# Attention: one plain 32-bit product for the second half of the probabilities in two of nine steps

## The chip, the core and the metric

The kernel runs on one core of a Trainium2 chip. The metric is the device time of one execution in microseconds. The engines are named as the profile names them: PE (matmuls, PEld its weight loads), DVE (VectorE), ACT (ScalarE), POOL (GpSimd) and SP (SyncE, which here only issues DMAs).

## What is computed

One layer of a hybrid network over 2048 latent and 256 context tokens: a projection, a gated linear attention (GLA) and a softmax attention side by side, an output projection, and a feed-forward block. The change is in the softmax attention, which the reference computes like this, with 8 query heads, 2 key/value heads (so 4 query heads share one) and a head size of 64:

```python
def blocked_attention(q, k, v):
    ...
    def one_block(qi):
        s = jnp.einsum('bqhgd,bkhd->bhgqk', qi.astype(F32), k.astype(F32))
        p = jax.nn.softmax(s, axis=-1)
        return jnp.einsum('bhgqk,bkhd->bqhgd', p, v.astype(F32))
```

Latent queries read 2048 latent and 256 cached keys; context queries read the 256 context keys. Everything is in 32-bit floats.

## The kernel before

The stages run one after the other; attention takes the stretch from about 280 to 1095 us. Its work is cut into units: one tile of 128 query tokens and one key/value head, so that 4 heads x 128 tokens = 512 columns (`ROW`) go through at once. There are 32 latent units and 4 context units. A latent unit has nine steps (`NS`), numbered j = 0 to 8 in the code and first to ninth here; a step takes two key tiles of 128 keys, its two halves, i = 0 and 1. Line numbers in this section are those of the kernel before.

Precision is kept by splitting. A number is rounded to a shorter format (fp32r) and the rest is kept as a second number. Keys and queries are split that way, and `vals` holds in its 128 columns the rounded values (64) and their rests (64). The probabilities are split while the kernel runs. For each step:

- PE makes the scores of each half in two products (L840, L841) into one of three banks `p_s`.
- ACT takes the exponential of each half into `prob` (L945, 128 x 512), then rounds both halves in one instruction into `thi` (L950, 128 x 1024).
- POOL subtracts: `tlo` = `prob` - `thi` (L781, 128 x 1024). In the third and the seventh step (`FOLDED`) it first adds the two halves of `prob` into `fold` (L779).
- DVE adds the probabilities up in `p_sum` (L1017, L1020), one step behind the scores: two adds in most steps, one (of `fold`) in the folded ones.
- PE multiplies the values with `thi` and with `tlo` (L854, L855) into `p_o`, for each half, three steps behind the scores: the products of the third step are issued in the sixth, those of the seventh in the first step of the next unit.

`prob`, `thi` and `tlo` have six slots (`SLOTS_P`), so a slot comes round after six steps. Beside this PE computes for the next unit the maxima over the keys in 18 "pieces" (L805, and L811 for the 256 cached keys), which DVE reduces (L993, L996) from two banks `p_r` used in turn; the plan of how many pieces go with which step is a list of numbers (`PLAN`). The same two banks serve the transposes of the maxima (L820), the row sums (L875, of which DVE takes the reciprocal, L1043) and their spread over the columns (L868). When a unit's products are done, in the third step after it (the fourth of the next unit), ACT copies half of `p_o` to `osb` (L930), and DVE adds the halves (L1039). In the sixth step of some units (`CHUNK_STEP`) PE also computes a piece of the modulation (L898).

Each engine works through its instructions in the order of the code and waits on semaphores. On PE a step is: scores of half 0, transposes and sums if due, values of half 0, a piece, scores of half 1, a piece, values of half 1, what pieces are left, the chunk.

Of the kernel before, what the change touches and what calls it, by code (L numbers as in the profile page):

```python
# [7 lines left out]
F32 = mybir.dt.float32  # L8
F32R = mybir.dt.float32r
U32 = mybir.dt.uint32  # L10
ALU = mybir.AluOpType
ACT = mybir.ActivationFunctionType
# [544 lines left out]
def attention(nc, g):  # L557
# [11 lines left out]
    ROW = 4 * P  # L569
# [6 lines left out]
    PLAN_FIRST = [3, 2, 1, 2, 2, 3, 3, 2, 0]  # L576
    AHEAD = 2
    FOLDED = (2, 6)
    BANKS = 3
    ADDS = 2 * NS - len(FOLDED)  # L580

# [8 lines left out]
    with ExitStack() as stack:  # L590
        ph = Phase(nc, stack, "att")
        s = ph.s
# [11 lines left out]
        prob = ph.sb("prob", [P, SLOTS_P, 2 * ROW])  # L604
        thi = ph.sb("thi", [P, SLOTS_P, 2 * ROW], F32R)
        tlo = ph.sb("tlo", [P, SLOTS_P, 2 * ROW], F32R)
# [16 lines left out]
        p_o = [ph.ps("p_o0"), ph.ps("p_o1")]  # L623
# [19 lines left out]
        def adds_before(b, j, i):  # L643

            folded = sum(1 for f in FOLDED if f < j) if b.nds > 1 else 0
            return b.a0 + (2 * j - folded + i)

        def bank_of(b, j, i):
            return p_s[(2 * b.step_no[j] + i) % BANKS]

# [77 lines left out]
        with nc.Block() as block:  # L728
# [40 lines left out]
            @block.gpsimd  # L769
            def _(pool):  # L770
                def step(S):
                    if S.now:
                        e, j = S.now
                        sl = e.step_no[j] % SLOTS_P
                        if e.nds > 1 and j in FOLDED:
                            f = FOLDED.index(j)
                            pool.wait_ge(s.ex, (e.g0 + (j + 1)) * 2)
                            wait(pool, s.sum, adds_before(e, j, 1) - ADDS)
                            pool.tensor_tensor(fold[:, f, :], prob[:, sl, 0:ROW], prob[:, sl, ROW:2 * ROW], ALU.add).then_inc(s.fold, 1)  # L779
                        pool.wait_ge(s.hi, e.g0 + (j + 1))  # L780
                        pool.tensor_tensor(tlo[:, sl, :], prob[:, sl, :], thi[:, sl, :].bitcast(F32), ALU.subtract).then_inc(s.lo, 1)  # L781

                schedule(step)

            @block.tensor
            def _(pe):
                pe.wait_ge(s.ckl, 1)
                for t in range(2):
                    for n in range(4):
                        last = pe.transpose(p_s[t][:, n * P:(n + 1) * P],  # L790
                                            ckp[:, t, n // 2, 2 * (n % 2):2 * (n % 2) + 2, :].rearrange("p a d -> p (a d)").bitcast(F32),
                                            g.ident[:, :])
# [30 lines left out]
                def step(S):  # L823
                    for v, i, item in S.early:
                        piece(v, i, item)
                    late = S.now and S.now[0].nds > 1
                    if S.turn and not late:
                        turn(*S.turn)
                    pieces = list(S.max)

                    def scores(i):
                        e, j = S.now
                        half = (e.g0 + j) * 2 + i
                        if j == 0 and i == 0:
                            pe.wait_ge(s.aux, e.n + 1)
                            pe.wait_ge(s.q[e.q], e.q_round * 32 + 32)
                        wait(pe, s.ex, half - (BANKS - 1))
                        bank = bank_of(e, j, i)
                        kt = slice((e.kt0 + 2 * j + i) * P, (e.kt0 + 2 * j + i + 1) * P)
                        pe.matmul(bank[:, :], g.keysT[:, e.kv, 0, kt], qa[:, e.q, :], start=True, stop=False)  # L840
                        pe.matmul(bank[:, :], g.keysT[:, e.kv, 1, kt], qb[:, e.q, :], start=False, stop=True).then_inc(s.st, 1)  # L841

                    def values(i):
                        b, j = S.val
                        if i == 0:
                            pe.wait_ge(s.lo, b.g0 + (j + 1))
                            if j == 0:
                                wait(pe, s.osum, b.n - 1)
                                if S.after is not None:
                                    pe.wait_ge(s.mod, S.after[0] * 2 + (S.after[1] + 1))  # L850
                        sl = b.step_no[j] % SLOTS_P
                        v = g.vals[:, (b.kt0 + 2 * j + i) * KVH + b.kv, :]
                        cols = slice(i * ROW, (i + 1) * ROW)
                        pe.matmul(p_o[b.kv][:, :], v, thi[:, sl, cols], start=j == 0 and i == 0, stop=False)  # L854
                        last = pe.matmul(p_o[b.kv][:, :], v, tlo[:, sl, cols], start=False, stop=j == b.nds - 1 and i == 1)  # L855
                        if i == 1:
                            last.then_inc(s.pv, 1)

                    if S.now:
                        scores(0)  # L860
                    if S.turn and late:
                        turn(*S.turn)
                    if S.turn_sums:
                        b, (bank, before) = S.turn_sums
                        pe.wait_ge(s.lb, b.n + 1)
                        pe.wait_ge(*before)
                        for n in range(2):
                            last = pe.transpose(bank[:, n * P:(n + 1) * P], lb[:, 2 * n:2 * n + 2, :].rearrange("p h d -> p (h d)"), g.ident[:, :])  # L868
                        last.then_inc(s.tsums, 1)
                    if S.fin:  # L870
                        b, (bank, before) = S.fin
                        pe.wait_ge(s.sums_out, b.n + 1)
                        pe.wait_ge(*before)
                        for h in range(G4):
                            last = pe.matmul(bank[:, h:h + 1], sums[:, b.kv, h * P:(h + 1) * P], ones[:, 0:1], start=True, stop=True)  # L875
                        last.then_inc(s.ls, 1)
                    if S.val:
                        values(0)
                    if pieces:
                        piece(*pieces.pop(0))  # L880
                    if S.now:
                        scores(1)
                    if len(pieces) > 1:
                        piece(*pieces.pop(0))
                    if S.val:
                        values(1)
                    for p in pieces:
                        piece(*p)
                    if S.chunk is not None and S.now[1] == CHUNK_STEP:

                        (e, j), (c, half) = S.now, S.chunk
                        wait(pe, s.osum, e.n)
                        pe.wait_ge(s.aw, c * 16 + 16)
                        pe.wait_ge(s.cpad, 1)
                        for k in range(KC):
                            for q in range(4):
                                col = half * HALF + q * QUART
                                last = pe.matmul(p_o[1 - e.kv][q * COLS:(q + 1) * COLS, 0:QUART], cpad[:, k, :], aw[:, k, col:col + QUART],  # L898
                                                 start=k == 0, stop=k == KC - 1)
                        last.then_inc(s.chunk, 1)  # L900
# [4 lines left out]
            def _(act):  # L905
# [11 lines left out]
                def step(S):  # L917
# [3 lines left out]
                    if S.summed:  # L921
                        b = S.summed
# [3 lines left out]
                    if S.fin:  # L926
                        b = S.fin[0]
# [3 lines left out]
                    if S.store:  # L931
                        b = S.store
                        act.wait_ge(s.oo, b.n + 1)
                        act.dma_start(g.mix_tile(b.qt)[:, (4 + 2 * b.kv) * P:(6 + 2 * b.kv) * P], oo[:, b.kv, :]).then_inc(s.out[b.kv], 16)
                    if S.now:
                        e, j = S.now
                        sl = e.step_no[j] % SLOTS_P
                        for i in range(2):
                            act.wait_ge(s.st, (e.g0 + j) * 2 + (i + 1))
                            if i == 0:  # L940
                                wait(act, s.lo, e.g0 + (j - SLOTS_P + 1))
                                before = S.reuse
                                if before is not None:
                                    act.wait_ge(s.sum, adds_before(*before, 2 if before[0].nds == 1 or before[1] not in FOLDED else 1))
                            act.activation(prob[:, sl, i * ROW:(i + 1) * ROW], bank_of(e, j, i)[:, :], ACT.Exp).then_inc(s.ex, 1)  # L945
                            if i == 0 and S.turn and late:
                                turn(*S.turn)
                        act.wait_ge(s.ex, (e.g0 + (j + 1)) * 2)
                        wait(act, s.pv, e.g0 + (j - SLOTS_P + 1))
                        act.activation(thi[:, sl, :], prob[:, sl, :], ACT.Copy).then_inc(s.hi, 1)  # L950
                    if S.fin:
                        b = S.fin[0]
                        act.wait_ge(s.rec, b.n + 1)
# [1769 lines left out]
```

## Time and profile before

| | us |
|---|---|
| median of 3 runs | 3373.76 (3371.11 to 3375.86) |
| span of the profiled execution | 3368.3 |
| PE busy | 3177.4 (94%) |
| DVE busy | 2376.2 (71%) |
| ACT busy | 1711.1 (51%) |
| POOL busy | 1711.3 (51%) |
| mean granted clock of PE | 0.973 |

The profiled execution's own time is its span, from the first to the last instruction; the runs' median is 5.5 us above it. Busy times are unions of the instructions of an engine over the whole kernel, so they mix attention with stages in which POOL and ACT do little. A matmul is drawn from its start to a modelled end, and the next one starts before that end; how fast PE goes is read from the distance between starts.

### The profile page before, as it was taken

The page shows a single profiled execution, that of the slowest core. Times are in us where ns is not written, and L with a number is a line of the kernel's source. Part 1 is how long each engine was busy: PE and PEld are TensorE (multiplying, and loading weights), DVE is VectorE, ACT ScalarE, POOL GpSimd, SP SyncE. Part 2 cuts the span into 40 slices and gives each one's busy share as a digit, 9 for nine tenths or more (in the row PEclk, how much of TensorE's full clock was granted, in tenths as well). Part 3 has the DMA queues.
Part 4 walks back from the last instruction along what each step waited for, and adds up shares of the span by engine and source line. Part 5 has one row for each costly group of instructions (what it writes and reads, how often), then busy time and mean ns, then how long its engine had stood idle before and what let it go on. Part 6 is the DMA issues. An engine that isn't in the chain of part 4 may idle for free. (4 is left out here: it accounts for less than half of the span.)

```text
span 3368.3 us, 48426 instructions
## 1 busy us (share of the span) xinstructions
PE 3177.4 (94%) x18066; PEld 2778.6 (82%) x18066; DVE 2376.2 (71%) x3262; ACT 1711.1 (51%) x2475; POOL 1711.3 (51%) x910
## 2 busy tenths in 40 slices
PE   6988999999998799998899699999999999899998
PEld 5975777777776798887688699999999999788886
DVE  4877999999996575339633588888888887222367
ACT  5865888888887585211244433443343433211122
POOL 2655999999997011111023377756776775000001
PEclk8998999999999899999999799999999999999999
DMA  6432011111100444338575567767785775655476
GB/s 218 157 121 75 29 50 45 48 48 46 50 21 22 139 159 148 111 95 257 176 222 183 189 191 234 234 175 235 223 247 157 228 227 149 214 200 180 176 256 223
DMA packets 431529, 518.42 MB, mean 154 GB/s; under 512 B 40112, under 2 KB 322048, under 8 KB 431296
## 3 DMA queue, kind: packets, MB, share of 16 engines
q1 hardware_dynamic: 384224, 412.21, 38.5%
q10 hardware_dynamic: 43968, 91.86, 7.9%
q0 software_dynamic: 3104, 11.27, 0.8%
q8 instruction: 144, 2.36, 0.3%
q14 instruction: 89, 0.73, 0.1%
HBM read 341.62 MB, written 173.64 MB: 153 GB/s over the span
## 5 line engine op out<-in xcount | busy, mean ns | idle before, releaser
L781 POOL TENSOR_TENSOR att_tlo<-att_prob,att_thi 128x1024 fp32r<-128x1024 f32 x292 | 694.0, 2406 | 62.9 <-ACT att_thi L950 62.9
L166 PE MATMUL fu_p<-fu_hhi,fu_whi 128*128 128x384 f32 x1848 | 620.7, 336 | 27.1 <-PEq L111 17.9
L167 PE MATMUL fu_p<-fu_hlo,fu_whi 128*128 128x384 f32 x1848 | 619.6, 335 | 0.0
L168 PE MATMUL fu_p<-fu_hhi,fu_wlo 128*128 128x384 f32 x1848 | 619.6, 335 | 0.0
L945 ACT ACTIVATE att_prob<-att_p_s 128x512 f32<-128x512 f32 x584 | 340.9, 591 | 87.1 <-PE att_p_s L841 81.0
L166 PEld LDWEIGHTS fu_p<-fu_hhi,fu_whi 128*128 128x128 f32 x1848 | 348.7, 189 | 30.1 <-issue 18.2
L993 DVE TENSOR_REDUCE att_mx<-att_p_r 128x1 f32<-128x512 f32 x512 | 341.7, 684 | 44.7 <-PE att_p_r L805 43.6
L167 PEld LDWEIGHTS fu_p<-fu_hlo,fu_whi 128*128 128x128 f32 x1848 | 348.8, 189 | 0.0
L168 PEld LDWEIGHTS fu_p<-fu_hhi,fu_wlo 128*128 128x128 f32 x1848 | 348.7, 189 | 0.0
L950 ACT ACTIVATE att_thi<-att_prob 128x1024 fp32r<-128x1024 f32 x292 | 309.7, 1061 | 9.3
L1807 POOL TENSOR_TENSOR fu_wsum<-fu_ws 128x1024 f32<-128x1024 f32 x66 | 177.0, 2682 | 240.6 <-DMA fu_ws<-in_w_ffn_dram 134.8
L1020 DVE TENSOR_TENSOR att_p_sum<-att_p_sum,att_prob 128x512 f32<-128x512 f32 x420 | 291.0, 693 | 8.3 <-DVE att_p_sum L1017 0.5
L2511 DVE TENSOR_TENSOR fd_alo<-fd_src,fd_ahi 128x1408 fp32r<-128x1408 f32 x62 | 100.8, 1626 | 259.2 <-ACT fd_ahi L2490 259.2
L2350 DVE TENSOR_TENSOR fu_wlo<-fu_wsum,fu_whi 128x1024 fp32r<-128x1024 f32 x132 | 219.1, 1660 | 83.3 <-ACT fu_whi L2269 82.6
L2269 ACT ACTIVATE fu_whi<-fu_wsum 128x1024 fp32r<-128x1024 f32 x132 | 140.0, 1060 | 252.8 <-PE fu_p L168 252.8
L854 PE MATMUL att_p_o<-att_thi,vals 128*128 128x512 f32 x584 | 240.9, 412 | 1.3 <-POOL att_tlo L781 1.3
L2459 POOL TENSOR_TENSOR fd_rs<-fd_ms,neg_half 128x1 f32<-128x1 f32 x18 | 10.1, 562 | 453.1 <-DVE fd_ms L2551 453.1
L2350 DVE TENSOR_TENSOR fu_wlo<-fu_ws,fu_whi 128x1024 fp32r<-128x1024 f32 x98 | 204.2, 2083 | 45.6 <-ACT fu_whi L2269 45.1
L2269 ACT ACTIVATE fu_whi<-fu_ws 128x1024 fp32r<-128x1024 f32 x98 | 104.0, 1061 | 258.7 <-PE fu_p L168 245.2
L840 PE MATMUL att_p_s<-att_qa,keysT 128*128 128x512 f32 x584 | 233.7, 400 | 0.7 <-ACT att_qb L915 0.7
L805 PE MATMUL att_p_r<-keysT,att_qa 128*128 128x512 f32 x512 | 220.7, 434 | 14.5 <-DVE att_mx L993 8.7
L855 PE MATMUL att_p_o<-att_tlo,vals 128*128 128x512 f32 x584 | 232.3, 398 | 0.0
(363 smaller groups left out, 7899.2 us busy)
## 6 DMA issues: line engine op xcount, KB each, us to landing
fu_ws<-in_w_ffn_dram SPq DMA_DIRECT2D x132, 512.0 KB, 8.0
gated_d<-fu_out SPq DMA_DIRECT2D x99, 448.0 KB, 5.5
fd_src<-gated_d SPq DMA_DIRECT2D x63, 704.0 KB, 4.1
second_d<-fu_hs ACTq DMA_DIRECT2D x77, 512.0 KB, 3.6
fu_hs<-in_w_ffn_dram ACTq DMA_DIRECT2D x121, 256.0 KB, 4.1
fd_second<-second_d SPq DMA_DIRECT2D x40, 512.0 KB, 5.8
fd_w<-second_d SPq DMA_DIRECT2D x37, 512.0 KB, 5.2
ga_h<-hT_d SPq DMA_DIRECT2D x36, 512.0 KB, 4.2
```

The lines of the kernel that those rows point to most:

```text
L166: pe.matmul(out, ah, bh, start=first, stop=False)
L167: pe.matmul(out, ah, bl, start=False, stop=False)
L168: return pe.matmul(out, al, bh, start=False, stop=last)
L781: pool.tensor_tensor(tlo[:, sl, :], prob[:, sl, :], thi[:, sl, :].bitcast(F32), ALU.subtract).then_inc(s.lo, 1)
L840: pe.matmul(bank[:, :], g.keysT[:, e.kv, 0, kt], qa[:, e.q, :], start=True, stop=False)
L854: pe.matmul(p_o[b.kv][:, :], v, thi[:, sl, cols], start=j == 0 and i == 0, stop=False)
L945: act.activation(prob[:, sl, i * ROW:(i + 1) * ROW], bank_of(e, j, i)[:, :], ACT.Exp).then_inc(s.ex, 1)
L950: act.activation(thi[:, sl, :], prob[:, sl, :], ACT.Copy).then_inc(s.hi, 1)
L993: dve.tensor_reduce(mx[:, v.kv, h, c:c + 1], bank[:, :], AX.X, ALU.max).then_inc(s.mx, 1)
L1020: dve.tensor_tensor(p_sum[:, :], p_sum[:, :], half, ALU.add).then_inc(s.sum, 1)
L2269: act.activation(whi[:, n % RING], source(c, i), ACT.Copy).then_inc(s.w_hi, 1)
L2350: dve.tensor_tensor(wlo[:, n % RING], source(c, i), whi[:, n % RING].bitcast(F32), ALU.subtract).then_inc(s.w_lo, 1)
```

## The change

In the latent units, in the third and the seventh step (`EXACT`, the same two steps as the folded ones), the second half of the probabilities is not split any more. ACT rounds and POOL subtracts only the first 512 columns in these steps. PE multiplies the second half's values with `prob` itself, both read as plain 32-bit floats, in one product in the place of two. Since PE now reads `prob`, ACT also waits, before it writes over such a slot, until the values product of the step that used it is done.

```diff
     FOLDED = (2, 6)
+    EXACT = (2, 6)
...
+        def exact(b, j, i):
+
+            return b.nds > 1 and i == 1 and j in EXACT
+
+        def split_cols(b, j):
+            return slice(0, ROW if exact(b, j, 1) else 2 * ROW)
+
...
+                        cols = split_cols(e, j)
                         pool.wait_ge(s.hi, e.g0 + (j + 1))
-                        pool.tensor_tensor(tlo[:, sl, :], prob[:, sl, :], thi[:, sl, :].bitcast(F32), ALU.subtract).then_inc(s.lo, 1)
+                        pool.tensor_tensor(tlo[:, sl, cols], prob[:, sl, cols], thi[:, sl, cols].bitcast(F32), ALU.subtract).then_inc(s.lo, 1)
...
-                        pe.matmul(p_o[b.kv][:, :], v, thi[:, sl, cols], start=j == 0 and i == 0, stop=False)
-                        last = pe.matmul(p_o[b.kv][:, :], v, tlo[:, sl, cols], start=False, stop=j == b.nds - 1 and i == 1)
+                        if exact(b, j, i):
+                            last = pe.matmul(p_o[b.kv][:, :], v.bitcast(F32), prob[:, sl, cols], start=False, stop=j == b.nds - 1)
+                        else:
+                            pe.matmul(p_o[b.kv][:, :], v, thi[:, sl, cols], start=j == 0 and i == 0, stop=False)
+                            last = pe.matmul(p_o[b.kv][:, :], v, tlo[:, sl, cols], start=False, stop=j == b.nds - 1 and i == 1)
...
+                                    if exact(before[0], before[1], 1):
+                                        act.wait_ge(s.pv, before[0].g0 + before[1] + 1)
...
-                        act.activation(thi[:, sl, :], prob[:, sl, :], ACT.Copy).then_inc(s.hi, 1)
+                        cols = split_cols(e, j)
+                        act.activation(thi[:, sl, cols], prob[:, sl, cols], ACT.Copy).then_inc(s.hi, 1)
```

On PE, in the sixth step of a unit, from the scores of its second half to the chunk, the order before is this (`att_p_o` is `p_o`, `att_p_r` a bank of `p_r`):

```order
L840 MATMUL att_p_s<-att_qa,keysT 128x512
L841 MATMUL att_p_s<-att_qb,keysT 128x512
L805 MATMUL att_p_r<-keysT,att_qa 128x512
L854 MATMUL att_p_o<-att_thi,vals 128x512
L855 MATMUL att_p_o<-att_tlo,vals 128x512
L805 MATMUL att_p_r<-keysT,att_qa 128x512
L898 MATMUL att_p_o<-att_aw,att_cpad 32x64 x32
```

The same place in the changed kernel:

```order
L849 MATMUL att_p_s<-att_qa,keysT 128x512
L850 MATMUL att_p_s<-att_qb,keysT 128x512
L814 MATMUL att_p_r<-keysT,att_qa 128x512
L864 MATMUL att_p_o<-att_prob,vals 128x512
L814 MATMUL att_p_r<-keysT,att_qa 128x512
L910 MATMUL att_p_o<-att_aw,att_cpad 32x64 x32
```

Two products between two pieces have become one; nothing else on PE changes place.

On ACT, from the second step of a unit to the fourth, with the copy `att_osb` for the unit before it, the order before is this:

```order
L950 ACTIVATE att_thi<-att_prob 128x1024
L925 ACTIVATE att_sums<-att_p_sum 128x512
L945 ACTIVATE att_prob<-att_p_s 128x512 x2
L950 ACTIVATE att_thi<-att_prob 128x1024
L945 ACTIVATE att_prob<-att_p_s 128x512 x2
L950 ACTIVATE att_thi<-att_prob 128x1024
L930 ACTIVATE att_osb<-att_p_o 64x512
L945 ACTIVATE att_prob<-att_p_s 128x512 x2
```

In the changed kernel:

```order
L965 ACTIVATE att_thi<-att_prob 128x1024
L937 ACTIVATE att_sums<-att_p_sum 128x512
L959 ACTIVATE att_prob<-att_p_s 128x512 x2
L965 ACTIVATE att_thi<-att_prob 128x1024
L959 ACTIVATE att_prob<-att_p_s 128x512 x2
L965 ACTIVATE att_thi<-att_prob 128x512
L942 ACTIVATE att_osb<-att_p_o 64x512
L959 ACTIVATE att_prob<-att_p_s 128x512 x2
```

The rounding right ahead of `att_osb` is half as long; the order is the same.

On POOL the changed kernel has, from the fold of one unit's third step on, these rows:

```order
L787 TENSOR_TENSOR att_fold<-att_prob 128x512
L790 TENSOR_TENSOR att_tlo<-att_prob,att_thi 128x512
L790 TENSOR_TENSOR att_tlo<-att_prob,att_thi 128x1024 x4
L787 TENSOR_TENSOR att_fold<-att_prob 128x512
L790 TENSOR_TENSOR att_tlo<-att_prob,att_thi 128x512
L790 TENSOR_TENSOR att_tlo<-att_prob,att_thi 128x1024 x3
```

The subtraction behind each fold, 128x1024 before, covers 512 columns now; the fold still stands ahead of it.

## Rows read from the trace of the kernel before

**Rows 1.** The page's costliest group: count, busy us, mean ns, idle before.

```profile
L781 POOL TENSOR_TENSOR att_tlo<-att_prob,att_thi 128x1024 fp32r<-128x1024 f32 x292 | 694.0, 2406 | 62.9 <-ACT att_thi L950 62.9
```

**Rows 2.** Busy us of PE, PEld, DVE, ACT, POOL in 30 units; L854 there.

```profile
304.05:1035.66 731.61, 723.50 (x4142) 551.91 (x4143) 673.22 (x1186) 640.87 (x931) 713.66 (x331) 1.00 0.13 43
...
L854 PE MATMUL att_p_o<-att_thi,vals x540: 389/397/484, 304.5 to 1034.5; 128*128 128x512 f32 x180
```

**Rows 3.** Who waited for whom, 304 to 1035: us, times, longest.

```profile
PEld att_p_r L805 <- DVE att_mx L993: 36.3, 107, 0.6
...
PEld att_p_r L805 <- DVE att_rec L1043: 14.2, 30, 0.5
...
PEld att_p_r L811 <- DVE att_mx L993: 8.5, 15, 0.6
```

**Rows 4.** Timeline of PE, first step of a unit: start, duration in us.

```profile
648.26 0.39 PE L854 MATMUL att_p_o<-att_thi,vals 128*128 128x512 f32 x1
648.49 0.40 PE L855 MATMUL att_p_o<-att_tlo,vals 128*128 128x512 f32 x1
...
648.97 0.39 PE L840 MATMUL att_p_s<-att_qa,keysT 128*128 128x512 f32 x1
```

**Rows 5.** Timeline, all engines, second to fourth step.

```profile
652.83 1.06 ACT L950 ACTIVATE att_thi<-att_prob 128x1024 fp32r<-128x1024 f32 x1
...
655.16 1.06 ACT L950 ACTIVATE att_thi<-att_prob 128x1024 fp32r<-128x1024 f32 x1
655.26 0.95 PE L875 MATMUL att_p_r<-att_ones,att_sums 128*128 128x1 f32 x8
...
656.07 0.48 PE L854 MATMUL att_p_o<-att_thi,vals 128*128 128x512 f32 x1
...
656.24 0.60 ACT L930 ACTIVATE att_osb<-att_p_o 64x512 f32<-64x512 f32 x1
656.33 1.28 POOL L779 TENSOR_TENSOR att_fold<-att_prob 128x512 f32<-128x512 f32 x1
...
657.56 0.40 PE L855 MATMUL att_p_o<-att_tlo,vals 128*128 128x512 f32 x1
657.58 2.39 POOL L781 TENSOR_TENSOR att_tlo<-att_prob,att_thi 128x1024 fp32r<-128x1024 f32 x1
657.75 0.18 DVE L1043 RECIPROCAL att_rec<-att_p_r 128x4 f32<-128x4 f32 x1
657.85 0.67 DVE L1020 TENSOR_TENSOR att_p_sum<-att_p_sum,att_fold 128x512 f32<-128x512 f32 x1
...
657.99 0.50 PE L805 MATMUL att_p_r<-keysT,att_qa 128*128 128x512 f32 x1
...
658.32 0.40 PE L840 MATMUL att_p_s<-att_qa,keysT 128*128 128x512 f32 x1
```

**Rows 6.** Timeline of PE, sixth step of that unit.

```profile
661.27 0.48 PE L854 MATMUL att_p_o<-att_thi,vals 128*128 128x512 f32 x1
661.60 0.39 PE L855 MATMUL att_p_o<-att_tlo,vals 128*128 128x512 f32 x1
662.15 0.50 PE L805 MATMUL att_p_r<-keysT,att_qa 128*128 128x512 f32 x1 [0.17 <-DVE att_mx L993]
...
663.41 0.40 PE L855 MATMUL att_p_o<-att_tlo,vals 128*128 128x512 f32 x1
663.68 0.50 PE L805 MATMUL att_p_r<-keysT,att_qa 128*128 128x512 f32 x1
```

**Rows 7.** Timelines of PE: plain 32-bit products of 64 and 128 columns.

```profile
296.86 1.10 PE L898 MATMUL att_p_o<-att_aw,att_cpad 128*32 128x64 f32 x64
297.89 0.50 PE L840 MATMUL att_p_s<-att_qa,keysT 128*128 128x512 f32 x1
...
1626.30 0.61 PE L1701 MATMUL ga_p_b<-states,go_qp 128*128 128x128 f32 x4
...
1627.19 0.61 PE L1701 MATMUL ga_p_b<-states,go_qp 128*128 128x128 f32 x4
```

## The prediction

> **What bounds the kernel now.** I read first where the changed code runs. Only attention is touched, and in it only the latent units; the page's costliest group [rows 1] makes POOL's split `tlo` (292 times 2.41 us) look like the resource that the change relieves. The second view is the busy time over 30 latent units (there are 540 high products in it, 18 a unit) [rows 2]: 731.61 us, so 24.39 us a unit. Of that POOL is busy 713.66 (97.5%), DVE 673.22, ACT 640.87, and PE's 723.50 is overstated because matmuls overlap. Share alone cannot decide between POOL and PE, so the third view is who waited for whom in the same stretch [rows 3]. PE's weight loads waited for DVE (36.3 us for the maxima, 14.2 for the reciprocal, 8.5 in the 256-column pieces) and for no POOL instruction at all. So POOL is busy, but nobody waits for it there.
>
> The timeline says why. PE issues 512-column products back to back: in the first step of a unit they start at 648.26, 648.49 and, two further on, 648.97 [rows 4], 0.23 to 0.24 us apart although each is drawn 0.40 long; I use 0.233. POOL's result is used late: the values product of a step is issued three steps after its scores. The tightest case is the step with the fold: POOL's `tlo` of the third step begins at 657.58 and takes 2.39, ending at 659.97 [rows 5]; the product that reads it starts at 661.27 [rows 6]. That leaves 1.30 us of slack where it is smallest.
>
> PE therefore sets the pace, with two or three short waits a unit. First wait: after the product at 657.56 the next piece should start 0.23 later, at 657.79, but starts at 657.99 [rows 5], because its bank is freed by DVE's reciprocal (657.75 plus 0.18). The one after it follows at 658.32, 0.33 instead of 0.23 later, so this wait costs 0.20 + 0.10 = 0.30 us. Its origin is ACT: rounding of the third step (655.16, 1.06 long), `osb` right behind it at 656.24, then two adds of DVE, then the reciprocal. Second wait: 661.60 to 662.15 [rows 6], 0.32 over the pace and again 0.10 behind it, for DVE, which is back to back there. Third: 663.41 to 663.68, 0.04 over, and 0.10 behind. One unit in two has another for the 256-column pieces (8.5 us in 15 waits [rows 3], weight-load time, which contains more than the delay).
>
> **The change, part by part.** All counts are for 32 latent units, two changed steps in each, 64 in all.
>
> *PE, removed:* two products of 512 columns each, 0.233 apart, 0.466 us together. *PE, added:* one product whose two operands are plain 32-bit values. The trace has no 512-column product of this kind, so I bound it. In the GLA stage such products have 128 columns, and each stands as two matmul records: eight records, four products, take from 1626.30 to 1627.19 [rows 7], 0.222 us a product. Four times that is 0.89 us for 512 columns. These rows do not prove the scaling, because the products with a single column also stand as two records and also take 0.10 us a record (655.26 to 656.07 for 8) [rows 5]: a weight load alone may fill that time. The second kind has 64 columns, four side by side on 32 columns of the array each: 64 records in 1.03 us (296.86 to 297.89) [rows 7], eight rounds, 0.129 a round, and 512 columns would take eight rounds, 1.03 us. Here the weights are small (32 columns), and a round of 64 columns still takes 0.129 us, where the pace of [rows 4] would give 0.029: about four times as slow, so the streaming itself is slower, not only the weight load. So the bounds are 0.466 (as cheap as what it replaces) and 1.03; I take 0.88, near the 128-column row, since both kinds speak for a product about four times as slow as a rounded one. The added price is 0.41 us a product, 0.82 a unit.
>
> The Trainium skill states the same reason as a rule: FP8 and Floating Point Precision, TensorE Precision Notes, has true FP32 go through the array in four passes. With the pace in TensorE: Matmul & The Clock Gate (columns over 2.4 GHz plus about 2.5 ns, 216 ns at 512) an estimate from these pages is 0.86 for the added product, 0.43 for the removed pair, and 0.43 more a product. The trace's 0.233 is slower than the page's 0.216. By the pages the sum would be 64 times 0.43, 27.5 us, before any wait is absorbed.
>
> *ACT:* the rounding of a changed step covers 512 columns instead of 1024. The nearest row is `osb`, also 512 columns, at 0.60 against 1.06 [rows 5], so 0.46 less, twice a unit. ACT waits for PE elsewhere, so this is worth something only where someone waits for ACT: at `osb`, the first wait above.
>
> *POOL:* `tlo` of a changed step halves, 1.1 to 1.2 us less (the fold, 128x512, takes 1.28 [rows 5]), 2.3 a unit. With 1.30 us of slack at the tightest place it buys PE nothing. The half comes behind the fold, so the fold is not earlier for it either. *ACT's new wait* for the values product before a slot is overwritten is for a step six back, whose product was issued three steps back: nothing. If that cover were gone, ACT would stop until that product is out, 0.88 us at most.
>
> Now put them in the order in which they meet, times being delays against the trace before. (a) The product of the seventh step is issued in the next unit's first step, where PE runs without a gap [rows 4]: +0.41. (b) The scores of the second and third steps come 0.41 later, so ACT's rounding of the third starts 0.41 later and is 0.46 shorter; `osb` and the reciprocal stay where they are. PE arrives at 657.79 + 0.41 = 658.20, past 657.93, and does not wait: of the 0.41, 0.20 and the 0.10 behind it are absorbed, +0.11 is left. (c) POOL's `tlo` of the second step waits for ACT's rounding (652.83 plus 1.06 [rows 5]); it moves 0.41 later, with it the fold, from ending at 657.61 to about 658.0. DVE's add of the fold began at 657.85, so it now begins about 0.2 later, and DVE is back to back from there to the second wait: this sets PE's delay to +0.2 at 662.15. (d) The product of the third step, in the sixth: +0.41, at 663.2; the third wait (0.04 and 0.10) goes away. Left: 0.2 + 0.41 − 0.14, about +0.5. In the units with the fourth wait DVE has by then been pushed back by the same late piece, so it absorbs nothing.
>
> The sum is 0.52 us a unit, times 32 = 16.6 us: 3368.3 + 16.6 = 3384.9 for the profiled execution. The median of the runs lies 5.5 above the span, so 3390.
>
> **Rivals.** *Nothing is absorbed:* PE pays 0.82 in each unit. For it: DVE and ACT depend on PE's pieces and scores and may slip along with it. 32 times 0.82 is 26, time 3400. *More is absorbed:* DVE idles 1.9 us a unit [rows 2], and if it catches up before the second wait, PE keeps 0.2 a unit: 6 us, 3380. Against it: the fold is late, and DVE has no gap between fold and wait. *The 32-bit product is as cheap as the pair (this one ends faster):* then (a) and (d) are nothing, ACT's shorter rounding brings `osb` 0.46 forward, the first wait's 0.30 is gained, and DVE's stretch starts when the fold is ready (657.61 instead of 657.85), 0.24 earlier; −0.24 a unit, −8 us, 3366. Between its −0.24 and my +0.52 the sign turns at an added price of about 0.13, a product of 0.60 us. Against it: the 64-column rounds. *POOL is the bound after all (faster):* its work falls by 2.3 us a unit, and the unit shrinks until PE has no waits left: 24.39, less the 0.30, 0.42 and 0.14 of above and some 0.2 for the wait that every second unit has, plus 0.82, makes 24.15, −0.24 a unit, −8 us, 3366. Against it: not one wait for `tlo` among PE's in 30 units [rows 3].
>
> **How the numbers follow.** Forecast as worked out 0.62; nothing absorbed 0.15; more absorbed 0.12; cheap product 0.06; POOL the bound 0.05. The forecast's own range is 3384 to 3397 (added price 0.35 to 0.5, which gives 13 to 20 us, and a margin for the spread of the runs). The range 3377 to 3403 takes in the two absorption cases and the dearer product (1.03 would make it some 23 us, 3397), and leaves out both faster rivals. A difference under 0.2% (7 us) cannot be told from none on this kernel: faster 0.10, same 0.08 (half of the "more absorbed" case and some of the rest), slower 0.82.
>
> **What the profile after would show.** The product of `prob` and `vals` as 128 records of 512 columns, about 0.44 apart; if they are 0.23 apart, the cheap rival holds. A unit of 24.9 us instead of 24.39. POOL's busy share near 87%, with more waits for ACT and none of PE for POOL. The wait for the reciprocal gone from PE's list, that for the maxima kept. If PE's waits for DVE do not shrink, nothing was absorbed. The prediction fails if the 32-bit product does not cost about four passes, or if PE was held by POOL in a way that the waits do not show.

## The result and the profile after

| | before | changed |
|---|---|---|
| median of 5 runs, us | 3371.11 (3369.8 to 3375.86) | 3383.56 (3381.05 to 3388.7) |
| ratio | | 1.0031, 95% interval 1.0019 to 1.0043 |
| span of the profiled execution, us | 3368.3 | 3381.8 |

The change costs 0.31%, some 10 us by the ratio. The forecast was 16.6 us and slower, a time of 3390. The direction was right; the measured cost is about a third smaller than forecast, and the median of 3383.56 lies 0.4 us under the forecast's own range (3384 to 3397) and inside the wider one (3377 to 3403).

The length of a unit tells more than the median, since it is the same in all units. I take it from the transposes of the maxima that end one unit's search and stand once in a unit (L820 before, L829 after): from the second to the 32nd of them there are 30 units. Before: 304.05 to 1035.45, 24.38 us a unit. After: 306.53 to 1047.98, 24.72. The 0.335 us more, 32 times, is 10.7 us. The two kinds of unit differ: without the chunk of the modulation 23.98 before and 24.18 after (+0.20), with it 24.78 and 25.25 (+0.46). The profiled spans differ by 13.5; attention accounts for 10 of it, the rest lies in the stages behind, whose code did not change.

The busy time of PE, PEld, DVE, ACT and POOL over those 30 units answers to [rows 2]:

```profile
306.53:1047.98 741.45, 736.28 (x4141) 557.64 (x4141) 676.52 (x1185) 621.18 (x931) 652.28 (x330) 1.00 0.13 42
```

POOL is now busy 652.28 of 741.45 us, 88.0% in the place of 97.5%, and ACT has 0.65 us a unit less. Neither made the kernel faster. The waits of the same stretch (us in total, times, longest) answer to [rows 3]:

```profile
POOL att_tlo L790 <- ACT att_thi L965: 78.4, 150, 1.1
...
PEld att_p_r L814 <- DVE att_mx L1008: 43.5, 120, 0.6
...
DVE att_osum L1054 <- ACT att_osb L942: 6.6, 30, 0.2
...
PEld att_p_r L820 <- DVE att_mx L1008: 5.0, 15, 0.3
```

The reader is to see four things. The wait for the reciprocal, 14.2 us before, has no row any more. The wait ahead of the 256-column pieces (L811 before, L820 after) fell from 8.5 to 5.0. The weight loads' waits for the maxima rose from 36.3 to 43.5: 7.2 us of the 43.5 are 30 waits of 0.24 behind the plain product in the first step of a unit, where there was no such wait before; the load is held there while PE is busy with the product (the price below is read over just such a place), so this costs PE nothing. And what POOL saved has turned into POOL waiting for ACT (11.4 us before, 78.4 now, by the whole list of waits of each kernel): it has less to do and is handed its work no earlier. ACT's new wait, for the values product before it overwrites a slot of `prob`, cost nothing: no values product stands in ACT's list of waits.

**The price of the product.** PE's timeline where one of the 64 products stands without a chunk behind it:

```profile
557.96 1.02 PE L864 MATMUL att_p_o<-att_prob,vals 128*128 128x512 f32 x2
558.41 0.80 PE L814 MATMUL att_p_r<-keysT,att_qa 128*128 128x512 f32 x1
559.05 0.39 PE L849 MATMUL att_p_s<-att_qa,keysT 128*128 128x512 f32 x1
```

The product stands as two records (x2). From its start to that of the second instruction behind it are 559.05 − 557.96 = 1.09 us; take off one piece at 0.233 and 0.856 is left for the product, 0.39 more than the pair's 0.466. The 47 products that can be read in this way give 0.853 to 0.861, median 0.856. The piece's own start at 558.41 must not be read as its turn: it is stamped just after the product's second record starts, and is drawn 0.80 long because it includes the rest of the product.

**The fourth step,** one whole step of the chain that [rows 5] show:

```profile
662.70 0.63 ACT L965 ACTIVATE att_thi<-att_prob 128x512 fp32r<-128x512 f32 x1
...
663.36 0.59 ACT L942 ACTIVATE att_osb<-att_p_o 64x512 f32<-64x512 f32 x1
...
663.85 1.29 POOL L787 TENSOR_TENSOR att_fold<-att_prob 128x512 f32<-128x512 f32 x1
...
663.99 0.85 DVE L1054 TENSOR_TENSOR att_osum<-att_p_o,att_osb 64x256 f32<-64x256 f32 x2 [0.22 <-ACT att_osb L942]
...
664.87 0.18 DVE L1058 RECIPROCAL att_rec<-att_p_r 128x4 f32<-128x4 f32 x1
...
665.10 0.40 PE L867 MATMUL att_p_o<-att_tlo,vals 128*128 128x512 f32 x1
...
665.18 0.70 DVE L1035 TENSOR_TENSOR att_p_sum<-att_p_sum,att_fold 128x512 f32<-128x512 f32 x1
665.33 0.40 PE L814 MATMUL att_p_r<-keysT,att_qa 128*128 128x512 f32 x1
```

The rounding takes 0.63 and not 1.06, `osb` follows, and the reciprocal is done at 665.05, before PE's product at 665.10 has even begun. The piece behind it starts 0.23 later, at the pace. DVE's next add is held by the fold (663.85 plus 1.29 is 665.14, start 665.18).

**The sixth step** answers to [rows 6]:

```profile
668.95 0.39 PE L867 MATMUL att_p_o<-att_tlo,vals 128*128 128x512 f32 x1
669.51 0.50 PE L814 MATMUL att_p_r<-keysT,att_qa 128*128 128x512 f32 x1 [0.17 <-DVE att_mx L1008]
```

The second wait is as long as before, 0.56 from start to start (0.55 in [rows 6]); over the 30 units the median is 0.57 in both kernels.

### The profile page after: what moved, and what is told of

The parts are those of the page before. It is cut to its first block and busy times, and to the rows that moved or that the text cites. A ratio compares the mean times of both kernels' runs of the same rounds, so it can differ in the third digit from the quotient of the medians.

```text
span 3381.8 us, 48490 instructions
## 1 busy us (share of the span) xinstructions
PE 3190.5 (94%) x18066; PEld 2784.0 (82%) x18066; DVE 2383.8 (70%) x3262; ACT 1692.0 (50%) x2475; POOL 1644.3 (49%) x910
## 5 line engine op out<-in xcount | busy, mean ns | idle before, releaser
L790 POOL TENSOR_TENSOR att_tlo<-att_prob,att_thi 128x1024 fp32r<-128x1024 f32 (+1 forms) x292 | 627.2, 2154 | 135.3 <-ACT att_thi L965 133.9
L965 ACT ACTIVATE att_thi<-att_prob 128x1024 fp32r<-128x1024 f32 (+1 forms) x292 | 282.5, 967 | 9.3
L814 PE MATMUL att_p_r<-keysT,att_qa 128*128 128x512 f32 x512 | 241.0, 474 | 13.1 <-DVE att_mx L1008 8.5
L850 PE MATMUL att_p_s<-att_qb,keysT 128*128 128x512 f32 x584 | 231.6, 397 | 0.0
L2505 ACT ACTIVATE fd_ahi<-fd_src 128x1408 fp32r<-128x1408 f32 x62 | 85.6, 1381 | 286.8 <-PE fd_p L168 267.0
```

The costliest lines, as they stand in the source:

```text
L790: pool.tensor_tensor(tlo[:, sl, cols], prob[:, sl, cols], thi[:, sl, cols].bitcast(F32), ALU.subtract).then_inc(s.lo, 1)
L814: pe.matmul(bank[:, :], qa[:, v.q, h * P:(h + 1) * P], g.keysT[:, v.kv, 0, c * ROW:(c + 1) * ROW], start=True, stop=True).then_inc(s.piece, 1)
L965: act.activation(thi[:, sl, cols], prob[:, sl, cols], ACT.Copy).then_inc(s.hi, 1)
```

## The experiments

Theory A, as in the prediction: PE sets the pace; each plain product costs it 0.39 us; the shorter rounding removes the wait for the reciprocal, the delay from the products takes up other waits, and POOL's relief is worth nothing. Theory B: what POOL or ACT save, or PE's waits by themselves, offset the price evenly. Each kernel was timed beside runs of the kernel before on the same chip; ratios are to those. The length of a unit comes from one profiled execution of each kernel; two kernels below whose edits turn out to change nothing have 24.375 and 24.374 against the 24.380 of before, so it repeats to about 0.01.

**One of the two steps alone.**

```diff
-    EXACT = (2, 6)
+    EXACT = (2,)
```

> Only the third step of each latent unit has the plain 32-bit product and the half splits. Theory (PE sets the pace, the product costs 0.39 us more than the pair, and ACT's shorter rounding ahead of the copy osb removes the wait for the reciprocal): 0.30 gained at that wait, 0.24 kept until the second wait, 0.39 paid behind it and 0.13 of the third wait gained, so about 0 a unit, 3367 to 3372 us. Rival (each of the 64 products costs the same share of the loss): half of the changed kernel's loss, +5 us, 3376.

Ratio 0.9992 (0.9983 to 1.0002), median 3371.02 against 3370.28, 24.35 us a unit (−0.03). In the second kernel `EXACT = (6,)`:

> Only the seventh step has the plain product and the half splits. Theory: the product is issued where PE runs without a gap, and the rounding ahead of osb is long again, so the wait for the reciprocal moves with PE and absorbs nothing: +0.39 a unit, +12 us, 3383. Rival (each product costs the same share of the loss): +5 us, 3376.

Ratio 1.0038 (1.0024 to 1.0051), median 3384.50, 24.77 a unit (+0.39). So the same edit is free in one step and costs its full price in the other. The seventh step alone is as slow as both together: an even share per product is ruled out. The two kernels do not differ by the place of the product alone: the third step also brings the shorter rounding ahead of `osb`. The next two kernels take that apart. The waits in the kernel with the seventh step alone keep the row that the changed kernel lost:

```profile
PEld att_p_r L814 <- DVE att_rec L1058: 14.3, 30, 0.5
```

**The two halves of the change.** First the products without the half splits:

```diff
-            return slice(0, ROW if exact(b, j, 1) else 2 * ROW)
+            return slice(0, 2 * ROW)
```

> The plain products stay, but ACT and POOL split the whole 1024 columns in every step as before; the output is unchanged. Theory: without the shorter rounding nothing of the first 0.39 is absorbed, of the second 0.13 and in every other unit 0.25 more; 0.53 a unit, +17 us, 3388. Rival (PE's own waits are what absorbs, ACT has no part): as the changed kernel, +10 to +12 us, 3382.

Ratio 1.0053 (1.0039 to 1.0067), median 3389.86, 24.90 a unit (+0.52). The forecast was +0.53 a unit and 3388. The wait for the reciprocal is back, and so is the wait of DVE for `osb`:

```profile
DVE att_osum L1054 <- ACT att_osb L942: 19.5, 30, 0.7
...
PEld att_p_r L814 <- DVE att_rec L1058: 14.3, 30, 0.5
```

Then the half splits without the products:

```diff
                         if exact(b, j, i):
-                            last = pe.matmul(p_o[b.kv][:, :], v.bitcast(F32), prob[:, sl, cols], start=False, stop=j == b.nds - 1)
+                            cols = slice(0, ROW)
+                            pe.matmul(p_o[b.kv][:, :], v, thi[:, sl, cols], start=False, stop=False)
+                            last = pe.matmul(p_o[b.kv][:, :], v, tlo[:, sl, cols], start=False, stop=j == b.nds - 1)
```

> ACT and POOL as changed (half splits), PE with two rounded products as before, which read the first half's columns of thi and tlo in the place of the second half's: the second half of the probabilities is left out of the values product in these steps. Theory: POOL's relief is worth nothing, ACT's some 0.24 a unit: -8 us, 3363. Rival (POOL was the bound): the unit shrinks until PE has no waits left, -1.1 a unit, -35 us, 3336. Second rival (neither matters): 3371.

Ratio 0.9991 (0.9981 to 1.0001), median 3368.95 against 3370.28, 24.20 a unit (−0.18). The ratio alone does not separate this gain from none; the unit's length does: 0.18 less in 30 units, somewhat under the 0.24 that I had expected, and nowhere near what it would be if POOL were the bound. The two halves add up, +0.52 and −0.18, to the +0.335 of the whole. They also give the third step alone: the −0.18, and for its product 0.39 less what the third and the fourth wait take up (0.13 and, in every second unit, 0.24), is −0.04 against the −0.03 measured. That step is free because the product comes with ACT's relief.

**POOL's half alone.**

```diff
-                            last = pe.matmul(p_o[b.kv][:, :], v.bitcast(F32), prob[:, sl, cols], start=False, stop=j == b.nds - 1)
+                            pe.matmul(p_o[b.kv][:, :], v, thi[:, sl, cols], start=False, stop=False)
+                            last = pe.matmul(p_o[b.kv][:, :], v, tlo[:, sl, 0:ROW], start=False, stop=j == b.nds - 1)
...
-                        cols = split_cols(e, j)
+                        cols = slice(0, 2 * ROW)
                         act.activation(thi[:, sl, cols], prob[:, sl, cols], ACT.Copy).then_inc(s.hi, 1)
```

> Only POOL's subtraction is halved in the third and seventh step; ACT rounds all 1024 columns, PE makes two rounded products, the low one with the first half's columns of tlo (the second half's low part is left out of the product in these steps). Theory: nobody waits for POOL's tlo, so no change: 24.38 us a unit, 3370. Rival (part of the gain of the half splits is POOL's): up to -0.18 us a unit, -6 us, 3364.

Ratio 0.9997 (0.9989 to 1.0006), 24.375 a unit against 24.380. POOL's relief is worth nothing here, and the 0.18 of the half splits is ACT's.

**The dose.** `EXACT = tuple(range(9))`, all nine steps:

> All nine steps of each latent unit have the plain product and the half splits. Theory: 9 times 0.39 is 3.5 us a unit more for PE, of which the waits of before can absorb at most 1.1: +2.4 to +3.5 a unit, +77 to +112, 3447 to 3482. Rival (the loss goes by the number of products, 0.17 us each as in the changed kernel): +1.5 a unit, +48, 3418.

Ratio 1.0192 (1.0176 to 1.0208), median 3438.32, 26.66 a unit: +2.28, which 32 times is 73 us (65 by the ratio). That is under the lower end of theory A (+2.4 a unit, 77 us) and well over its rival (+1.5, 48). Nine prices of 0.39 are 3.50, so 1.22 us a unit were absorbed, where I had allowed 1.1. Adding up what the starts of PE's instructions in the kernel before exceed the pace by gives about 1.4 us in a unit without the chunk (of which the wait for the reciprocal 0.30, the second 0.43, the third 0.13, the one ahead of the 256-column pieces 0.30) and 0.3 less with it, some 1.2 on average. The two kinds of unit agree with this: those without the chunk grew from 23.98 to 26.04, so that 1.44 was absorbed, those with it from 24.78 to 27.27, which leaves 1.0. So nearly everything was absorbed that could be, and I had counted the waits too low. The second wait, for one, is gone in all 30 units (0.23 from start to start). This kernel's list still has 24.6 us in 90 waits of weight loads for the maxima, but all 90 stand behind a plain product, where the load is held while PE works on the product.

**The wait for the reciprocal without the change.** If that wait hangs on `osb`, moving the copy ahead of the rounding should give the same gain with every product rounded as before:

```diff
-                    if S.fin:
-                        b = S.fin[0]
+                    early = S.val is not None and S.val[1] == S.val[0].nds - 1
+
+                    def copy_half(b):
                         act.wait_ge(s.pv, b.g0 + b.nds)
...
+                        if early:
+                            copy_half(S.val[0])
                         act.wait_ge(s.ex, (e.g0 + (j + 1)) * 2)
                         wait(act, s.pv, e.g0 + (j - SLOTS_P + 1))
                         act.activation(thi[:, sl, :], prob[:, sl, :], ACT.Copy).then_inc(s.hi, 1)
```

(`early` is true in the step in which PE makes the last values product of a unit; `copy_half` is the old code of `osb`.)

> The kernel before, with ACT's copy osb put ahead of the rounding of the third step in the place of behind it; nothing else changes, the output is the same. Theory (the wait for the reciprocal hangs on that copy): the wait disappears, but DVE's add still has to wait for the fold, so the gain is that of the half splits, -0.18 to -0.24 a unit, -6 to -8 us, 3363. Rival (the gain of the half splits has another cause): 3370.

Ratio 0.9978 (0.9968 to 0.9988), median 3367.59 against 3373.14, 24.21 a unit (−0.175): the same as the half splits' −0.18. Now DVE waits for the fold, as expected:

```profile
DVE att_p_sum L1026 <- POOL att_fold L779: 14.2, 30, 0.5
```

**The rest of DVE's stretch.** In addition, one piece ahead of the add of the fold:

```diff
-                    if pieces and S.sum and S.sum[1] == 0:
+                    if pieces and S.sum and (S.sum[1] == 0 or S.sum[1] in FOLDED):
```

> As osb_early, and in the steps in which DVE adds the fold it reduces the first piece ahead of that add. Theory (PE's second wait is DVE's back-to-back stretch, whose start is held by the fold): the stretch starts earlier, and most of the waits for the maxima goes too, -0.5 to -0.8 us a unit, -16 to -25 us, 3350. Rival (DVE's stretch is bound by its own work, the start does not matter): as osb_early.

Ratio 0.9947 (0.9934 to 0.9960), median 3355.62 against 3373.14, 23.86 a unit (−0.52), the small end of the theory's −0.5 to −0.8. The second edit without the first:

> The kernel before with only the second edit of osb_early_piece_first: in the steps in which DVE adds the fold, it reduces the first piece ahead of that add. Theory (both must go together: the late copy osb holds the start of DVE's stretch, so the fold is not what it waits for): the wait for the reciprocal stays, 0 to -0.1 us a unit, 3368 to 3373. Rival (the order of piece and add is the whole gain): 3356.

Ratio 0.9997 (0.9986 to 1.0007), 24.37 a unit. It is worth 0.35 us a unit behind the first edit and nothing without it: the start of DVE's back-to-back stretch is held by two things in turn, first `osb`, then the fold. The busy times of the kernel with both edits (PE, PEld, DVE, ACT, POOL) show what is next:

```profile
305.02:1020.75 715.73, 711.32 (x4141) 556.88 (x4142) 671.64 (x1185) 634.16 (x930) 711.46 (x331) 1.00 0.13 44
```

POOL is busy 711.46 of 715.73 us, 99.4%, and here it does hold others up. In the units with a chunk its fold is late, DVE waits for it, and DVE's stretch and with it PE's second wait follow:

```profile
651.59 0.70 DVE L1026 TENSOR_TENSOR att_p_sum<-att_p_sum,att_fold 128x512 f32<-128x512 f32 x1 [0.33 <-POOL att_fold L779]
```

The fold of the third step ends 12.72 us after the transposes in these units and 12.24 after them in the units without a chunk (medians). The second wait is there in 14 of the 15 units with a chunk and in none of those without.

**The change on the better kernel.** Both edits and the third step alone (`EXACT = (2,)`):

> osb_early_piece_first, and the plain product with the half splits in the third step only. POOL was busy 99.4% of the 30 units of osb_early_piece_first and DVE waited for its fold there, so POOL's relief could be worth something now. Theory: PE's floor without waits (23.16 us a unit) plus 0.39 plus the few waits that no relief takes away is 23.8 to 23.95 against 23.86: 3354 to 3359. Rival (POOL bounds this kernel and its relief outweighs the product): under 23.7 a unit, 3350 or less.

Ratio 0.9931 (0.9917 to 0.9946), median 3350.24 against 3375.58, 23.78 a unit. It lies between the two theories' numbers: 0.08 us a unit better than without the product, though the product costs 0.39. The intervals of the two ratios (0.9934 to 0.9960 and 0.9917 to 0.9946) overlap, so that it is the faster one is shown by the unit's length alone, 2 us in all. The gain is where POOL was late: with the shorter subtraction the fold ends at 12.25 in the units with a chunk too, the second wait is gone in all 30 units (0.23 from start to start), and the units with a chunk are 0.17 shorter (24.46 to 24.29). Those without one, where POOL had not been late, are 0.02 longer; there waits further on take up the product's price (the fourth falls from 0.52 to 0.34 from start to start). So the rival's mechanism, POOL's relief, is real in this kernel, in half of the units, but is worth less than the rival's forecast. POOL is now busy 681.84 of 713.42 us, 95.6%.

Both edits and the whole change:

> osb_early_piece_first with the whole change (third and seventh step). Theory: fewer waits are left to absorb the 0.78 us of the two products: PE's floor 23.16 plus 0.78 plus 0.2 is 24.1 to 24.25 a unit against 23.86, +8 to +12 us on osb_early_piece_first, 3364 to 3368. Rival (what POOL and ACT save grows in worth as the kernel gets tighter): under +5 us, 3360 or less.

Ratio 0.9968 (0.9957 to 0.9979), median 3364.67, 24.17 a unit: +0.31 on the kernel with both edits, 10 us, as on the kernel before. This lies in the theory's ranges (24.1 to 24.25 a unit, 3364 to 3368).

The fastest version is the third step alone on top of both edits, 0.69% under the kernel before; the two edits by themselves, which leave every product as it was, give 0.53% of it.

## Why the prediction was right

The mechanism held in every step but one, and the sum took a number that its own steps do not give. The 3390 was 6.4 us too high. Attention was put 5.9 too high (16.6 against 10.7). The 5.5 us between a profiled span and the median was 1.8 (3381.8 and 3383.56): 1.8 is what every run has between its time and its span, the rest of the 5.5 had been the spread of the runs. Against these two, the stages behind attention, which the change does not touch, came out some 3 us longer in the profiled execution. That they hid half of attention's error is luck.

- *Who sets the pace:* right. POOL alone relieved changes nothing (24.375 against 24.380), though it was busy 97.5%; the products alone cost 0.52 us a unit.
- *The price, 0.41:* measured 0.39 (0.856 for the product; I had 0.88). The rival in which the product costs 0.466 is refuted by the timeline. By the pages of the Trainium skill named in the prediction (FP8 and Floating Point Precision, TensorE Precision Notes; TensorE: Matmul & The Clock Gate, Back-to-back issue gap) the estimate for the product was 0.86: the trace agrees. Their 0.43 for the pair does not agree with the 0.466 measured.
- *(a), the product of the seventh step costs its full price:* right; alone it costs +0.39 a unit.
- *(b), the shorter rounding keeps the reciprocal in place and the first wait goes:* right. The reciprocal ends 12.53 us after the unit's transposes (12.57 before; medians of 30 units). The wait is gone in the changed kernel and there with its 14.3 us in both kernels with a plain product whose rounding ahead of `osb` is long.
- *(c), the fold holds DVE, +0.2 at the second wait:* right in place and size. The second wait ends 16.99 us after the unit's transposes and ended 16.79 after them before (medians of 30 units), so +0.20. One premise was read a little wrong: before the change POOL's `tlo` of the second step followed at once on that of the first (it starts at 653.98, ACT's rounding had ended at 653.89), so it did not wait for ACT, and the fold moved by 0.37 in the place of 0.41.
- *(d), up to the third wait:* right: +0.20 + 0.39 − 0.13 = +0.46 behind it, and units with a chunk became 0.46 longer. The prediction's own terms, 0.2 + 0.41 − 0.14, make 0.47.
- *The sum:* it took 0.52 (0.82 less the first wait's 0.30 makes this number) and not the 0.47 of (d). The 0.05 are 1.6 us too much.
- *(d), the last sentence:* this step failed. I wrote "In the units with the fourth wait DVE has by then been pushed back by the same late piece, so it absorbs nothing". These units became only 0.20 longer: the fourth wait, 0.53 from start to start before, was 0.28 after and absorbed 0.24 us, 16 times, 4 us. This is most of the difference between 16.6 and 10.7 us; the slip in the sum is nearly all of the rest. With the two mended the same steps give 16 times 0.47 and 16 times 0.20, 10.7 us. The rival *more is absorbed* (0.2 a unit, 6 us) was right in size for every second unit, though the wait that absorbs is the fourth, not one ahead of the second.

Why DVE was not pushed back is in its timeline. Before the change, the late piece of the sixth step and DVE around it:

```profile
639.68 0.50 PE L805 MATMUL att_p_r<-keysT,att_qa 128*128 128x512 f32 x1
...
640.13 1.29 DVE L993 TENSOR_REDUCE att_mx<-att_p_r 128x1 f32<-128x512 f32 x2
```

and after it:

```profile
646.85 0.78 PE L814 MATMUL att_p_r<-keysT,att_qa 128*128 128x512 f32 x1
...
647.31 1.28 DVE L1008 TENSOR_REDUCE att_mx<-att_p_r 128x1 f32<-128x512 f32 x2
```

DVE reduces two pieces in a row there, and the late one is the second, some 0.6 us after the first (the first begins at 640.13, before the late piece's drawn end at 640.18): at 640.73 before, when it had been ready since 640.18. DVE was 0.55 us behind it, not waiting for it. After the change the piece is ready at 647.63 and DVE comes to it at 647.91, still 0.28 behind. Counted from each unit's transposes (621.35 and 628.34) the piece is ready 0.45 later, and DVE's reductions stand 0.18 later, no more than the late fold had already moved them: in these units DVE runs without a gap from the add of the fold to the fourth wait, before and after. The fourth wait is for such a reduction, so it ends 0.18 later too, and the 0.39 of the product falls into it:

```profile
642.67 0.30 PEld L811 LDWEIGHTS att_p_r<-keysT,att_qa 128*128 128x128 f32 x2 [0.57 <-DVE att_mx L993]
```

```profile
649.84 0.30 PEld L820 LDWEIGHTS att_p_r<-keysT,att_qa 128*128 128x128 f32 x2 [0.32 <-DVE att_mx L1008]
```

I had taken DVE for waiting on the piece because the two stand next to each other in time; the order of the pieces in the two banks says which one it reads.

## What to carry to other kernels

An engine at 97.5% whose results are used three steps later bounded nothing here: look for the wait on its output before relieving it, and look again when the kernel has become tighter, since at 99.4% the same engine held others up. A price put on the engine that sets the pace is absorbed only where that engine waits for something that does not slip along, so the same edit can be free in one step, where it also shortens work that the waits hang on, and cost all of its price in another; a forecast needs the place of each, and for each wait whose result the waiting engine reads next. A relief that seemed to come from the removed work (ACT's shorter rounding) can be had from the order alone here: one copy put ahead of one rounding gave the same gain, and opened the way to a larger one.

## What the runs showed of the hardware

A product of plain 32-bit operands with 512 columns took 0.856 us at a granted clock of 1.00, in two records 0.43 apart, against 0.233 for a rounded one: 3.7 times, and 1.84 times the rounded pair that it replaces. Its weight loads (0.19 each) are drawn beside matmuls, not between them. I had not expected the stamps: in the changed kernel the 512-column matmul behind such a product is recorded as starting 0.03 to 0.07 us after the product's second record, and as lasting 0.75 to 0.80, so that distances between starts must be read across both.
